# Sample attention: value products of the last batch directly behind its transposes, score products of the next batch last

## The reference, cut to what matters

```python
def _fox_sample(q, k, v, logf, ck, cv, clogf):        # 8 requests, 16 queries, 512 + 16 keys, 8 heads of 64
    k_all = jnp.concatenate([ck.astype(k.dtype), k], axis=1)
    v_all = jnp.concatenate([cv.astype(v.dtype), v], axis=1)
    lf_all = jnp.concatenate([clogf.astype(jnp.float32), logf], axis=1)
    c_t = jnp.transpose(jnp.cumsum(lf_all, axis=1), (0, 2, 1))
    cq = c_t[:, :, p_len:]
    sc = jnp.einsum('bqhd,bkhd->bhqk', q, k_all, preferred_element_type=jnp.float32) * scale
    sc = sc + cq[..., None] - c_t[:, :, None, :]
    sc = jnp.where(mask, sc, -jnp.inf)
    p = jax.nn.softmax(sc, axis=-1)
    return jnp.einsum('bhqk,bkhd->bqhd', p.astype(v_all.dtype), v_all)
```

## Time and profile before

| | us |
|---|---|
| median of 3 runs | 1916.54 (1915.13 to 1919.03) |
| the profiled execution's own time | 1914.82 |
| span of the profiled execution | 1913.0 |
| TensorE busy in the span | 1808.4 |
| sample attention, steps 0 to 7, first layer | about 362.6 to 415 |
| the same, second layer | about 1308.7 to 1361 |

### The profile page before, as it was taken

The page is one execution under the profiler, slowest core; times in us unless marked ns, Lnnn a source line. Parts: engine busy times, 40 slices in busy tenths (PEclk is TensorE's granted clock), DMA queues, the critical chain, the costliest instruction groups (busy, mean ns, idle before and its releaser), DMA issues.

```text
span 1913.0 us, 30260 instructions
## 1 busy us (share of the span) xinstructions
PE 1808.4 (95%) x10838; PEld 1542.3 (81%) x10838; DVE 888.6 (46%) x1432; ACT 540.2 (28%) x944; POOL 135.8 (7%) x360
## 2 busy tenths in 40 slices
PE   5999999899999999999979999998989999999997
PEld 4767795567999999999866677855679999999996
DVE  3325435443545555554534264355354555554454
ACT  3202325432322222222233033254233222222221
POOL 1102100000100000000011021001010000000000
PEclk9988999999899999999989999999999999999999
DMA  6203330253122222222231043204421222222223
GB/s 217 67 2 80 105 136 26 78 188 122 56 78 73 79 66 77 77 77 77 77 86 56 2 105 120 100 23 146 163 90 56 78 77 66 87 67 76 77 73 107
DMA packets 125860, 163.06 MB, mean 85 GB/s; under 512 B 25652, under 2 KB 77182, under 8 KB 125438
## 3 DMA queue, kind: packets, MB, share of 16 engines
q1 hardware_dynamic: 125192, 159.96, 27.5%
q10 hardware_dynamic: 576, 1.90, 0.2%
HBM read 152.31 MB, written 9.53 MB: 85 GB/s over the span
## 4 chain that ended last, share of the span: by engine, by line
PE 89%; DVE 3%; issue 2%; ACT 2%; DVEq 2%; DMA 1%; SPq 0%; POOL 0%; POOLq 0%; ACTq 0%
PE bank L1533 85%; PE bank L1595 4%; DMA raw<-in_w_in 1%; DMA raw<-in_w_out 1%; DVE kT L1419 1%; DVEq L1437 1%; ACT whi L875 1%; DVEq L1398 0%; DVE wlo L1098 0%; ACT ps L1034 0%; ACT kT L919 0%; DVE hlo L1107 0%; DVE xn L1116 0%; ACT xn L896 0%; DVEq L1253 0%
## 5 line engine op out<-in xcount | busy, mean ns | idle before, releaser
L1533 PE MATMUL bank<-hhi,whi 128*128 128x320 f32 (+1 forms) x1632 | 507.9, 311 | 5.0 <-DVE wlo L1098 5.0
L1533 PE MATMUL bank<-hlo,whi 128*128 128x320 f32 (+1 forms) x1632 | 506.9, 311 | 0.0
L1533 PE MATMUL bank<-hhi,wlo 128*128 128x320 f32 (+1 forms) x1632 | 506.9, 311 | 0.0
L1098 DVE TENSOR_TENSOR wlo<-raw,whi 128x1024 fp32r<-128x1024 f32 (+1 forms) x204 | 245.6, 1206 | 391.0 <-ACT whi L875 389.7
L875 ACT ACTIVATE whi<-raw 128x1024 fp32r<-128x1024 f32 (+1 forms) x204 | 211.9, 1041 | 487.7 <-PE bank L1533 459.1
L1533 PEld LDWEIGHTS bank<-hhi,whi 128*128 128x128 f32 (+1 forms) x1632 | 305.8, 187 | 8.2 <-DVE wlo L1098 5.6
L1533 PEld LDWEIGHTS bank<-hlo,whi 128*128 128x128 f32 (+1 forms) x1632 | 305.6, 187 | 2.7
L1533 PEld LDWEIGHTS bank<-hhi,wlo 128*128 128x128 f32 (+1 forms) x1632 | 305.5, 187 | 1.8
L1533 PE MATMUL bank<-whi,hhi 128*128 128x512 f32 x560 | 230.6, 412 | 4.9 <-DVE wlo L1098 4.0
L1533 PE MATMUL bank<-wlo,hhi 128*128 128x512 f32 x560 | 225.0, 402 | 0.0
L1533 PE MATMUL bank<-whi,hlo 128*128 128x512 f32 x560 | 224.8, 401 | 0.0
(11 more groups left out here) (198 smaller groups left out, 1687.4 us busy)
## 6 DMA issues: line engine op xcount, KB each, us to landing
raw<-in_w_in SPq DMA_DIRECT2D x55, 512.0 KB, 3.7
raw<-in_w_gate SPq DMA_DIRECT2D x44, 512.0 KB, 3.7
raw<-in_w_up SPq DMA_DIRECT2D x44, 512.0 KB, 3.8
raw<-in_w_down SPq DMA_DIRECT2D x44, 512.0 KB, 3.8
vb<-in_cache_fox_v SPq DMA_DIRECT2D x16, 1024.0 KB, 5.5
raw<-in_w_out SPq DMA_DIRECT2D x16, 512.0 KB, 5.4
kb<-in_cache_fox_k SPq DMA_DIRECT2D x8, 1024.0 KB, 6.2
kbo<-in_cache_fox_k SPq DMA_DIRECT2D x8, 1024.0 KB, 5.6
```

The lines of the kernel that those rows point to most:

```text
L1098: dve.tensor_tensor(wlo[:, s_, 0:w_], raw[:, s_, 0:w_], whi[:, s_, 0:w_].bitcast(F32), ALU.subtract).then_inc(lo_split, 1)
L1533: return pe.matmul(out, lhsT=lhsT, rhs=rhs, start=start, stop=stop, skip_group_check=True)
```

## The change

In TensorE's `step(n)`, part 4 (values of batch n-1) is moved ahead of part 3 (scores of batch n). Nothing else is altered; the streams of the other engines and of SyncE's DMAs are the same instruction for instruction. Step 0 has only parts 1 and 3, steps 8 and 9 have no part 3, so the order differs in steps 1 to 7, in each of the two layers.

```diff
                         transposes(key, parts, l)
+                    if 1 <= n <= NB:
+                        pe.wait_ge(v_in[w], l * 64 + 16 * ((n - 1) // 2 + 1))
+                        B.wait_taken(pe, ("pt", n - 1), l)
+                        B.wait_taken(pe, ("po", n), l)
+                        key = ("so", n - 1)
+                        B.wait_room(pe, key, l)
+                        for k in range(5):
+                            for p_ in range(4):
+                                c = slice(p_ * P, (p_ + 1) * P)
+                                ins = mm(bank[B.bank(key)][32 * p_:32 * p_ + 32, 0:P],
+                                         pTs[:, w, k * P + 32 * p_:k * P + 32 * p_ + 32],
+                                         vb[:, w, k, c] if k < 4 else fv[:, TS, c], k == 0, k == 4)
+                        fill(ins, key)
                     if n < NB:
                         pe.wait_ge(q_ready, l * NB + n + 1)
...
                         fill(mm(bn[:, 0:P], identb, maskb[:, (2 + n) * P:(3 + n) * P], False, True), new)
-                    if 1 <= n <= NB:
-                        pe.wait_ge(v_in[w], l * 64 + 16 * ((n - 1) // 2 + 1))
...
-                        fill(ins, key)
```

## The result

The changed kernel took 1945.09 us as the median of its first four runs (1939.65 to 1953.74), 1.0159 times the kernel before (interval 1.0116 to 1.0201). The runs of both kernels spread more than the three shown ahead of the prediction: beside the experiments the kernel before ran 40 more times in two sets (23 and 17), from 1907.1 to 1927.8 with a mean of 1916.75 (standard error 0.9), and the changed one ran 16 times in all, these four among them, from 1933.2 to 1953.7, mean 1943.1 (1.5), median 1942.4. The difference of the means is 26.4 us. The recorded time lies above the predicted range (1934.0 to 1943.5); the median over all 16 runs lies just inside it, and the forecast of 1939.2 was too low all the same.

A forecast was written before the change was run, and what follows sets the result against it. A loop of waits between engines was taken to bound the step; 12.56 us growth less 1.23 at the exit gave 11.33 per layer, 22.7 for both, so a median of 1939.2 us, range 1934.0 to 1943.5.

The forecast's parts named there:

- What bounds it: Sample attention: a 6.45 us loop of waits between TensorE, VectorE and ScalarE sets the step, without the value products.
- Leg 1: From a step's scores to the transposes of the next step's key pair 2; unchanged at 4.57 us.
- Leg 2: From key pair 2's transposes to the value products, which wait for VectorE's last os copy; 0.63 us of new wait.
- Leg 3: The value products until TensorE issues the scores; 1.23 us, including a gap of 0.20.
- the rival without a gap: No 0.20 us gap between values and scores, a step growing by 1.66 us; 1936.4 us, chance 0.14.
- Step 1: First reordered step of each layer, waiting for the pTs copy; grows by 0.17 + 1.23 = 1.40 us.
- the exit: End of step 7: first output slab starts 1.77 instead of 3.00 us after the scores, 1.23 us back per layer.
- The clock: Rival: new TensorE pauses make its clock fall, 9 us per layer costing 6.5 us in all; 1945.7 us, chance 0.07.
- the clock stays at 1.00: Expected sign: TensorE's granted clock does not fall in the changed loop, so nothing is added for it.
- The range: 8 in 10 for 1934.0 to 1943.5 us, the top holding a clock fall of 3 us in one layer.

The follow-up runs named there:

- kt_first: Changed kernel with ScalarE's copy of key pair 0 moved ahead of its exponentials and VectorE's copy of key pair 1 directly behind its maximum; 1916.44 us.
- after: The changed kernel as first measured and profiled, against the kernel before; median of four runs 1945.09 us.
- again: The changed kernel run again with no edit; 1940.97 us, 1.0114 times the kernel before.
- again2: The changed kernel run once more with no edit; 1941.77 us, 1.0135 times the kernel before.
- paused: Changed kernel with VectorE's two maxima of a step taken twice, lengthening TensorE's pause ahead of key pair 2; 1983.08 us.
- pts: Changed kernel with VectorE's copy to pTs signalled by its own semaphore, so value products in steps 2 to 8 skip the os copies; 1932.92 us, one run.
- first3: Kernel before with the new order in steps 1 to 3 alone; 1935.97 us, a single time.
- filled: Changed kernel with products that nothing reads put into TensorE's two new pauses, steps 2 to 7; 1939.51 us.
- filled2: Changed kernel with the pauses filled by products that nothing reads, run once more; 1936.78 us.
- last1: Kernel before with the new order in step 7 alone; 1921.10 us, a single time.
- ahead: Both copies moved as in kt_first; TensorE's order is scores, next key pairs 0 and 1, previous values, next pairs 2 and 3; 1910.94 us.
- ahead2: The kernel of ahead with the key loads split in two halves, the half for pairs 0 and 1 issued earlier; 1903.06 us.

## Why the prediction was right or wrong

- **What bounds it:** right. The loop of waits sets the step, and what was in the values' shadow came into it.
- **Leg 1 (4.57):** right, 4.58; kt_first shows that ScalarE's order makes it.
- **Leg 2 (2.51, with 0.63 of new wait):** right in size, 2.53. The releaser named (`os`) was right, by 0.13 us.
- **Leg 3 (1.23):** too large, 1.09. This was the rival without a gap: the score weights load directly behind the values' (their PEld row at 388.34 has no idle time before it), while the last value products, whose row runs from 388.23 to 388.66, are under way. The Trainium skill, "TensorE: Matmul & The Clock Gate", Part 2, says that weight loads are pulled ahead of products in flight where the target does not conflict. The trace agrees. The reason I had against this rival was no reason: in both places that gave 1.23, step 3 and step 8, a load of 128 columns follows the values, so they could not tell that the following shape does not matter.
- **Step 1 (+1.40) and the exit (-1.23):** 1.35 and -1.35. The sum for both layers is 21.0 in the traces and 21.3 in the runs, where I had 22.7.
- **The clock, the step that failed:** "the clock stays at 1.00" was given nearly all the weight, so that the sum has nothing for it, and its fall got 0.07 with the price of one 9 us stretch per layer, 6.5 us. I argued from one stretch of 10.8 us with a pause of 1.85 that stood alone; a loop that repeats such a pause 14 times met falls in 3 of its 6 stages seen (after, again, again2), and in none of four once the pauses were filled. In those three profiles the stages lost 1.3, 5.7 and 0 us. The averages over the runs say 5.0 (1.8) for the whole kernel. Whether all of that lies inside the stages the three profiles can't settle. That repeated pauses bring falls is best shown by paused, where the loss grew by 33 us, and by a count over all profiles: of the 12 stages that repeat a pause of 1.85 us or more (after, again, again2, pts, first3, paused) 9 have a granted clock below 1.00, of the 14 others (before, filled, filled2, kt_first, last1, ahead, ahead2) none. How much it costs the changed kernel rests on means less than three standard errors apart.
- **In numbers:** 1939.2, less 1.4 for the loop, 5.0 for the clock and 0.2 for the kernel before make 1943.0, the mean of the 16 runs. The first four happened to be 2.8 us above that in their mean and 2.0 in their median, and that part is luck.
- **The range:** made from three runs of before within 4 us of each other. The same kernel spreads over 20, nearly all of it with the granted clock.

## What to carry to other kernels

Here work that was written behind a producer, while the other engines worked on their long reply, cost the loop nothing; in front of the producer it cost its own length and the wait for its own operands, in every round. Before moving work, go round the loop by the order of each engine: here two copies ahead of the exponentials gained back all that the move had cost, and with the key transposes in the gap the loop came down to TensorE's own work (busy 38.45 of 39.75 us). And when a change turns TensorE's idle time from short to repeated, price the clock too: the mean granted clock of many runs tells it apart from the loop, and one profile does not.

## What the runs showed that was not expected

Products that nothing reads made the changed kernel faster, 1937.3 against 1943.1 us: span less loss stayed (1885.6 and 1885.7) and the clock's loss fell by 5.7. A pause longer by 0.9 us per step (1.85 to 2.8) cost 39.7 us where the loop explains 13: TensorE had 0.79 and 0.77 of its clock on average in the two stretches shown, that is, 1.2 GHz for two fifths of them and more. And the kernel before's runs in one set differ by 20 us, nearly all through the granted clock, whose mean goes from 0.969 in the slowest run to 0.978 in the fastest.
